# HGRN2's scores inside blocks of 32 and 64 tokens as small column-tiled matmuls

## The reference

```python
cum = jnp.cumsum(gc, axis=2)                                   # gc = log f, f in (0, 1), per token and dimension
diff = cum[:, :, :, None, :] - cum[:, :, None, :, :]
decay = jnp.where(tri, jnp.exp(jnp.where(tri, diff, 0.0)), 0.0)
scores = jnp.einsum('bhtk,bhsk,bhtsk->bhts', qc, kc, decay)    # q_t . k_s, decayed over the tokens between
o = scores @ vc + (qc * exp(cum)) @ S                          # S: state carried from chunk to chunk
```

## Time and profile before

| | |
|---|---|
| timed runs, median (range) | 966.26 us (964.32 to 968.34) |
| profiled execution: its span, first to last instruction | 961.5 us |
| median of the runs less that span | 4.8 us |
| TensorE matmul busy | 932.1 us, 97% |
| VectorE busy | 691.0 us, 72% |
| ScalarE busy | 518.4 us, 54% |
| GpSimd busy | 371.8 us, 39% |
| loads | 162.57 MB, mean 169 GB/s |

### The profile page before, as it was taken

How to read it: one execution, slowest core, us unless ns; L and a number is a source line. 1 busy time by engine, 2 the same in 40 slices (tenths; PEclk the granted TensorE clock), 3 DMA queues, 4 the chain that set the end, 5 groups by cost and what they waited for, 6 DMA issues and landing times.

```text
span 961.5 us, 15057 instructions
## 1 busy us (share of the span) xinstructions
PE 932.1 (97%) x6110; PEld 846.5 (88%) x6110; DVE 691.0 (72%) x886; ACT 518.4 (54%) x790; POOL 371.8 (39%) x136
## 2 busy tenths in 40 slices
PE   7999999999999999999999999999999999999996
PEld 7998986888888878999999999899899888888885
DVE  4998586788884257657688987876645589999722
ACT  6853466544544356655535346555545566666532
POOL 0000000565664410001645542755676345665541
PEclk9999999999999999999999999999999999999998
DMA  9662432755555645445533425344356455555551
GB/s 360 209 214 80 151 129 97 278 176 181 194 196 180 213 154 180 174 157 184 186 108 117 147 89 153 132 135 159 109 182 212 149 197 181 200 189 180 193 197 45
DMA packets 30437, 162.57 MB, mean 169 GB/s; under 512 B 9089, under 2 KB 9489, under 8 KB 11936
## 3 DMA queue, kind: packets, MB, share of 16 engines
q1 hardware_dynamic: 30304, 161.53, 48.7%
q0 software_dynamic: 64, 0.08, 0.0%
HBM read 160.48 MB, written 1.12 MB: 168 GB/s over the span
## 4 chain that ended last, share of the span: by engine, by line
PE 86%; DVE 8%; ACT 3%; DMA 2%; issue 1%; SPq 1%; DVEq 0%; ACTq 0%
PE ring L1582 27%; PE acc L1660 18%; PE acc L1594 9%; PE ring L1594 9%; PE ring L1613 5%; PE acc L1595 4%; PE ring L1595 4%; PE acc L1837 3%; DMA raw<-wstream 2%; PE acc L1695 1%; DVE w_lo L1026 1%; DVE y L1078 1%; ACT w_hi L631 1%; PE ring L1695 1%; DVE ret_inv L1189 1%
## 5 line engine op out<-in xcount | busy, mean ns | idle before, releaser
L594 POOL TENSOR_TENSOR w_lo<-raw,w_hi 128x1024 fp32r<-128x1024 f32 x124 | 358.3, 2894 | 569.5 <-ACT w_hi L631 569.3
L631 ACT CAST w_hi<-raw 128x1024 fp32r<-128x1024 f32 x284 | 296.8, 1051 | 325.2 <-PE ring L1582 127.8
L1026 DVE TENSOR_TENSOR w_lo<-raw,w_hi 128x1024 fp32r<-128x1024 f32 x160 | 198.2, 1250 | 103.2 <-ACT w_hi L631 93.3
L1582 PE MATMUL ring<-h,w_hi 128*128 128x256 f32 x1408 | 257.4, 285 | 5.6 <-DVE w_lo L1026 3.1
L1582 PEld LDWEIGHTS ring<-h,w_hi 128*128 128x128 f32 x1408 | 219.7, 192 | 8.1 <-issue 6.4
L1582 PE MATMUL ring<-h,w_lo 128*128 128x256 f32 x704 | 199.1, 283 | 0.0
L1582 PEld LDWEIGHTS ring<-h,w_lo 128*128 128x128 f32 x704 | 135.0, 192 | 0.0
L1594 PE MATMUL acc<-h,w_hi 128*128 128x512 f32 x352 | 124.7, 397 | 0.8 <-DVE h L1084 0.8
L1594 PE MATMUL ring<-h,w_hi 128*128 128x512 f32 x352 | 124.2, 396 | 0.0
L1595 PE MATMUL acc<-h,w_lo 128*128 128x256 f32 x352 | 98.2, 279 | 0.0
L1595 PE MATMUL ring<-h,w_lo 128*128 128x256 f32 x352 | 98.2, 279 | 0.0
(11 more groups left out here) (255 smaller groups left out, 1395.8 us busy)
## 6 DMA issues: line engine op xcount, KB each, us to landing
raw<-wstream SPq DMA_DIRECT2D x142, 1024.0 KB, 4.9
toep_t<-toep SPq DMA_DIRECT2D x16, 96.0 KB, 3.1
x<-x_tok SPq DMA_DIRECT2D x2, 512.0 KB, 4.9
mem<-mem_tok SPq DMA_DIRECT2D x1, 1024.0 KB, 11.7
w_ple<-wproj SPq DMA_DIRECT2D x1, 1024.0 KB, 7.0
out_t<-y SPq DMA_DIRECT2D x4, 256.0 KB, 2.4
decay<-decay_tab SPq DMA_DIRECT2D x1, 768.0 KB, 6.5
gain_mix_pre<-gains SPq DMA_DIRECT2D x1, 512.0 KB, 6.2
```

What stands on the lines that cost most here:

```text
L594: nc.gpsimd.tensor_tensor(w_lo[:, u % UNITS], unit_of_raw(u), as_f32(w_hi[:, u % UNITS]), ALU.subtract).then_inc(lo_ready["pool"], 1)
L631: nc.scalar.copy(w_hi[:, u % UNITS], unit_of_raw(u)).then_inc(hi_ready, 1)
L1026: V.tensor_tensor(w_lo[:, u % UNITS], unit_of_raw(u), as_f32(w_hi[:, u % UNITS]), ALU.subtract).then_inc(lo_ready["dve"], 1)
L1582: last = mm(dst, w[a], src[:, b, kt], start=n == 0 and i == 0, stop=n == kts - 1 and i == 2)
```

## The change

- The diagonal is computed for blocks of 32 tokens: 64 calls with 32 weight columns and 32 streamed columns, each to its own 32 PSUM partitions, all in one bank. ScalarE copies the bank once, to a compact tile `st_near` of 512 columns (the space of `prod_tmp`).
- Levels 1 to 16 have the same shape (64 calls, one bank each, the banks taken in turn). One masked copy of 128x512 per level brings them into `st_near`; the masks are 32 columns wide and are loaded as 160 columns in place of 896.
- Level 32 (64 calls of 32 columns) and level 64 (32 calls of 64 columns, two banks) compute only the wanted blocks, straight from `k_f`, `k_b`, `q_f`, `q_b`. They have no key copies and no masks.
- ScalarE spreads the scores into `st_hg`: `spread_near` after the last masked level, `spread_far` after levels 32 and 64, each in copies of 32 or 64 partitions with 512 elements a lane, 12 in all.
- `f_f` and `f_b` are one tile, and their product in `grow` is one instruction.
- The cross scores wait for these copies (`st_far`) and for all masked ones.

```diff
-        f_f = at(0, "f_f", HG, S)
-        f_b = at(8, "f_b", HG, S)
+        f_fb = at(0, "f_fb", 2 * HG, S)
+        f_f, f_b = f_fb[:, 0:HG], f_fb[:, HG:]
...
+        st_near = prod_tmp[:].rearrange("p a (n c) -> p (a n) c", c=32)
...
+        def near(lo, n, shift=0):
+            v = st_hg[lo:lo + n].rearrange("p a (b c) -> p a b c", c=P)
+            return v[:, :, 0:4:3, lo % P + shift:lo % P + shift + n]
+
+        def level_bank(i):
+            return sc[(i + 1) % 4]
...
-                if side in LEVEL_AFTER:
+                if LEVEL_AFTER.get(side, MASKED) < MASKED:
                     level_keys(LEVEL_AFTER[side])
...
             def diagonal():
-                for g in range(4):
-                    act.wait_ge(sc_done, SC_LEVEL + g + 1)
-                    nc.scalar.copy(diag_view(g), sc[g][:].rearrange("p (a b c) -> p a b c", a=2, b=2)
-                                   ).then_inc(st_diag, 1)
+                act.wait_ge(sc_done, SC_LEVEL + 1)
+                nc.scalar.copy(st_near.rearrange("p a c -> p (a c)"), sc[0][:]).then_inc(st_diag, 1)
+
+            def spread_near():
+                act.wait_ge(st_mask, MASKED)
+                for lo in range(0, P, 32):
+                    nc.scalar.copy(near(lo, 32), st_near[lo:lo + 32].rearrange("p (a b) c -> p a b c", b=2))
+
+            def spread_far(i):
+                b = LEVELS[i]
+                act.wait_ge(sc_done, SC_LEVEL + 1 + i + 1)
+                banks = [sc[2]] if b == 32 else [sc[3], sc[0]]
+                heads = HG // len(banks)
+                for n, bank_ in enumerate(banks):
+                    for lo in range(0, P, b):
+                        shift = b if lo % (2 * b) == 0 else -b
+                        ins = nc.scalar.copy(near(lo, b, shift)[:, heads * n:heads * n + heads],
+                                             bank_[lo:lo + b].rearrange("p (a b c) -> p a b c", b=2, c=b))
+                    ins.then_inc(st_far, 1)
...
             def masks(i):
-                for g in range(4):
-                    dve.wait_ge(sc_done, SC_LEVEL + 4 * (i + 1) + g + 1)
...
-                    ins.then_inc(st_mask, 1)
+                dve.wait_ge(sc_done, SC_LEVEL + 1 + i + 1)
+                if i >= MASKED:
+                    return
+                if i == 0:
+                    dve.wait_ge(st_diag, 1)
+                c = CONST["mask"] + 32 * i
+                m = con[:, c:c + 32].bitcast(I32).unsqueeze(1).to_broadcast([P, 2 * HG, 32])
+                src = level_bank(i).rearrange("p (a c) -> p a c", c=32)
+                V.copy_predicated(st_near, m, src).then_inc(st_mask, 1)
...
-                V.tensor_tensor(fa[:, :, 0:1], fa[:, :, 0:1], fb_[:, :, 0:1], ALU.mult)
-                V.tensor_tensor(ba[:, :, 0:1], ba[:, :, 0:1], bb_[:, :, 0:1], ALU.mult).then_inc(level_ready, 1)
+                ga, gb = halves(f_fb[:])
+                V.tensor_tensor(ga[:, :, 0:1], ga[:, :, 0:1], gb[:, :, 0:1], ALU.mult).then_inc(level_ready, 1)
...
             def level(i):
                 b = LEVELS[i]
+                w = max(b, 32)
                 pe.wait_ge(level_ready, i + 1)
...
+                if i == 3:
+                    pe.wait_ge(st_diag, 1)
+                if i >= 4:
+                    pe.wait_ge(st_mask, 2 * i - 8 if i == 6 else i - 3)
+                for hd in range(HG):
+                    if i < MASKED and hd % 4 == 0:
+                        pe.wait_ge(mix_keys, 2 * i + hd // 4 + 1)
+                    out_ = level_bank(i + hd // 4 if b == 64 else i)
+                    for tt in range(2):
+                        c = w * ((2 * hd + tt) % (512 // w))
+                        for lo in range(0, P, w):
+                            t = tt * P + lo
+                            if b < 32:
+                                keys = k_mix[hd // 4][:, hd % 4, t:t + w]
+                                queries = partners(q_b[:, hd, t:t + w], b)
+                            elif lo % (2 * b) == 0:
+                                keys, queries = k_f[:, hd, t:t + w], q_f[:, hd, t + b:t + 2 * b]
+                            else:
+                                keys, queries = k_b[:, hd, t:t + w], q_b[:, hd, t - b:t]
+                            last = mm(out_[lo:lo + w, c:c + w], keys, queries, start=True, stop=True)
+                last.then_inc(sc_done, 1)
```

More of the change, by code:

```diff
@@ L172 @@
 LEVELS = [1, 2, 4, 8, 16, 32, 64]
-NCONST = 3 * P + len(LEVELS) * P
+MASKED = 5
+NCONST = 3 * P + MASKED * 32
 def lo_count(u, who):
@@ L373, in program @@
         st_mask = sem("st_mask")
+        st_far = sem("st_far")
         st_cross = sem("st_cross")
@@ L466, in program @@
         SC_LEVEL = 2 * RET
-        SC_CROSS = SC_LEVEL + 4 * (1 + len(LEVELS))
+        SC_CROSS = SC_LEVEL + 1 + len(LEVELS)
         SC_HGO = SC_CROSS + 4
-        def diag_view(g):
-            v = st_hg[:, 2 * g:2 * g + 2].rearrange("p a (b c) -> p a b c", c=P)
-            return v[:, :, 0:4:3]
+        def near(lo, n, shift=0):
[3 more added lines that the diff above has]
+            return sc[(i + 1) % 4]
         SIDE_FILLS = [(name, j) for name, j, _, _ in FILLS if name in ("hi", "hg", "nq", "nk", "nv", "cq")]
@@ L904, in _ @@
                     diagonal()
+                if LEVEL_AFTER.get(e) == MASKED:
+                    spread_near()
+                if LEVEL_AFTER.get(e, 0) >= MASKED:
+                    spread_far(LEVEL_AFTER[e])
                 if e == CROSS_AFTER:
@@ L1361, in grow @@
                 nb = HG * S // (2 * b)
-                fa, fb_ = halves(f_f[:])
-                ba, bb_ = halves(f_b[:])
+                fa, fb_ = halves(f_f)
+                ba, bb_ = halves(f_b)
                 bc = lambda t: t[:, :, 0:1].to_broadcast([P, nb, b])
@@ L1812, in diagonal @@
                 pe.wait_ge(level_ready, 1)
[L1813 to L1819, removed]
+                for hd in range(HG):
+                    for tt in range(2):
+                        c = 32 * (2 * hd + tt)
+                        for lo in range(0, P, 32):
+                            t = slice(tt * P + lo, tt * P + lo + 32)
+                            last = mm(sc[0][lo:lo + 32, c:c + 32], ksum[:, hd, t], q_s[:, hd, t], start=True, stop=True)
@@ L1841, in cross @@
+                last.then_inc(sc_done, 1)
             def cross():
                 pe.wait_ge(level_ready, 1 + len(LEVELS))
+                pe.wait_ge(st_mask, MASKED)
+                pe.wait_ge(st_far, 3)
                 for g in range(4):
-                    pe.wait_ge(st_mask, 4 * (len(LEVELS) - 1) + g + 1)
                     for a in range(2):
@@ L2050, in host_layout @@
     con = [np.eye(P, dtype=f)] + [np.full((P, P), 1.0 / n, f) for n in (512, 128)]
[L2051 to L2054, removed]
+    for b_ in LEVELS[:MASKED]:
+        row, colm = idx[:, None] % 32, idx[None, :32]
+        con.append(((row // (2 * b_) == colm // (2 * b_)) & (row // b_ != colm // b_)).astype(f))
     con = np.concatenate(con, axis=1)
```

## The result

After the change the kernel takes 958.13 us (median of 4 runs, 957.12 to 960.41), the kernel before 966.98 us beside it (4 runs, 964.32 to 968.34). The ratio is 0.9929, 95% interval 0.9907 to 0.9951: faster by 8.9 us, where 20 were forecast. The profiled execution took 957.12 us with a span of 955.3.

What follows compares the result with a forecast made beforehand. TensorE, busy 97% of the span, was taken as the bound. In the stage 37.4 us becomes 14.0 + 2.0 = 16.0, gain 21.4, taken as 20: span 941.5, time 946.3 us, range 939 to 965.

Steps and rivals of the forecast that it cites:

- the 37.4 that the prediction read from the chain: TensorE's chain time for the scores in the stage, outside twelve weight fills; forecast to become 16.0 us.
- The bursts: Score matmuls on TensorE: 1.7 us for each of the first seven groups, 2.1 for level 64, 14.0 us against 29.
- The rival of no overlap: At the bursts, each small record loads, then streams, alone: 55 ns, 7.0 us a level, 987 us; chance 0.12.
- The four updates of 1.2 us stay.: VectorE's four updates per level were forecast to keep their 1.2 us each.
- the merged product: VectorE's f_f and f_b products as one: bounds 3.7 us (one delay) and 6.4 (both); 3.7 used at levels 4 and 8.
- The chain from a burst's end to the next burst: From a burst's end to the first half's keys: 10.3 us, under 11.5 of two fills, so level 4 and 8 gaps go.
- Ahead of level 64: VectorE's chain of 5.1 us, updates and product, hidden under a fill of 5.75; the gap of 1.14 us goes.
- Waits: TensorE's waits in the stage: of 8.4 us some 2.0 were forecast to remain.
- Level 2's: TensorE's wait ahead of level 2, 0.86 us, stays, its keys being queued on ScalarE behind a weight cast.
- The rival in which the gain gets stuck behind the other engines: Merged product of 6.4, slow 32-lane copies or late cast return 1 to 1.5 us per level: 956 us, chance 0.12.
- a wait of up to 1 us for instructions: At the first two groups, 512 instructions in 3 us, TensorE may wait up to 1 us; costed at nothing.
- Carrying 4.8 us around the span: The difference between the 961.5 us span and the 966.26 us median, carried over unchanged to the forecast time.

Runs made afterwards that it cites:

- the first experiment: The kernel after, with every w_lo subtraction of the fills hi 0 to cq 1 on VectorE in place of three in four on GpSimd: 944.90 us, ratio 0.9791.
- both variants of the kernel before: The kernel before, once with every subtraction of the fills hi 0 to cq 1 on VectorE, 964.52 us; once with the two decay products as one instruction, 961.62 us.

## Why the prediction was wrong

Stage, in us: forecast, measured in the kernel after, and in the first experiment.

| | before | forecast | after | all on VectorE |
|---|---|---|---|---|
| bursts and the waits ahead of them | 36.4 | 16.0 | 26.5 | 15.1 |
| stage, diagonal to cross scores | 106.1 | 84.7 | 97.7 | 86.6 |
| gain in the stage | | 21.4 | 8.4 | 19.5 |

(The measured columns are by starts of matmuls; that of before counts 1 us less than the 37.4 that the prediction read from the chain. The waits that the prediction lists add up to 6.8 us of its 8.4; by starts they are 8.0.)

**The bursts: right, and a bit cheap.** Forecast 1.7 us a level, 1.0 for streaming and 0.7 added; the steps of levels 4 to 32 take 1.32 us each in the first experiment, the change of tiling included. The starts lie within 1.10 us. Level 64 was forecast 2.1, and takes that too: its starts lie within 1.86 us, and the change of tiling adds 0.2; in the kernel after, at the low clock, they lie within 2.82. Eight bursts make about 11 us against 14.0. The rival of no overlap is out. The Trainium skill, TensorEngine Tiling (Array Packing), Instruction Overhead, gives every matmul some 60 cycles, by estimate 25 ns at 2.4 GHz; the measured 8.6 ns a record over four tiles is below that, and the measurement decides. Within one tile, with some 33 ns from start to start, it isn't tested here.

**The failed step: "The four updates of 1.2 us stay."** The forecast treated the long f_f and f_b as a property of the products, and bounded only the merged product (3.7 to 6.4 us). That product came out near it at the early levels, 4.4, 2.0 and 3.2 us. But the delay belongs to whatever VectorE runs on two SBUF inputs while GpSimd subtracts. Merging two delayed instructions removed one place to be delayed and moved the delay to the updates. The chain from a burst's end to the next burst, forecast at 10.3 us, is 14.8 before level 4, over the 11.5 us of two fills. Ahead of level 64 it was forecast at 5.1 us under one fill of 5.75, and is 9.1: the first update takes 3.21 us in place of 1.2, and the product, which has 64 elements a lane, 2.30 in place of 0.3. The update ends 1.1 us after a subtraction of GpSimd's, the product lies beside one. The two delays are 4.0 us, more than the 3.25 us of TensorE's wait.

**Waits: forecast 2.0 us, measured about 12.** Ahead of levels 2, 4, 8, 16, 32 and 64 TensorE waits 1.06, 3.23, 1.03, 1.83, 0.47 and 3.25 us, and 1.3 inside level 1 (0.45 for the second key copy, and a stop of 0.85, on which more below). Level 2's is what I said would stay. Those of levels 4, 8 and 64 were to go and didn't; those of 16 and 32, 0.2 us before, are all but new. The rival in which the gain gets stuck behind the other engines, at 956 us, came nearest in time, and in place (1 to 1.5 us a level). Its causes were wrong: neither a product of 6.4, nor slow 32-lane copies, nor a late cast.

**The clock: not in the forecast at all.** The two waits of 3.2 us took it down for 3.4 us each. Between starts the fills of the stage cost 1.4 us more than before. Two more falls, near 135 and 599 us, cost 1.6 and 1.5 us. The one at 135 isn't the change's: it stands behind a wait of 2.2 us that is the same in all 13 profiled executions, and came in 7 of them, both variants of the kernel before among them. The one at 599 stands behind a wait of 2.0 us that all 13 have too, and came in two of them. And 0.8 us were gained near 40 us, where a wait of 1.5 us for VectorE is missing. That wait comes and goes as well: the two variants of the kernel before, with the old constants, don't have it, and three variants of the kernel after do. These three take the stage's 8.4 to about the 6.2 us between the spans; by the medians it is 8.9.

**The rest.** ScalarE's copies are hidden, as forecast. The masked copies are five of 0.75 us against 0.7. The cross scores don't wait for VectorE's updates. The instruction queue went from 0.80 to 0.88 MB against 90 KB forecast. For the first two groups the forecast allowed a wait of up to 1 us for instructions, and something stops TensorE there:

```profile
476.72 0.62 PE L1870 MATMUL acc<-q_bf,k_mix 128*32 128x32 f32 x37 [0.85 <-issue]
```

The stop comes behind record 219 of the 256 of the diagonal and level 1, where the program waits for nothing. It stands at the same record in the kernel after and in all eight variants of it that keep the interleaved order, 0.5 to 1.8 us long, and not in the one ordered tile by tile, whose bursts are slower. That fits instructions that arrive late, but no run here shows the cause. Carrying 4.8 us around the span was wrong in a small way: the runs show 1.8 to 1.9 between span and time, so the profiled execution of before comes to some 963.3 us, under the three runs shown with it.

Taken together: the work removed from TensorE was worth about what I said, and became visible (944.9 us against the forecast 946.3) only when VectorE was let off its waits for GpSimd. That the two numbers lie so close is in part luck: the bursts are some 3 us cheaper than forecast there, the waits 2 us dearer, and the fills, with the stop at 506.6 us in one, 1.8 us dearer.

**Open.** The stop inside level 1, and the one inside a fill of the first experiment; why the clock falls behind the waits at 132 and 597 us in some executions and not in others.

## What to carry to other kernels

When an instruction is long for its elements, find what it collides with before costing it: a delay that belongs to two engines doesn't go with the instruction that shows it, it moves to the next one in its place. Work that reads PSUM can be the cover under which GpSimd runs for free; if you shrink it, redo the timetable of GpSimd, or try giving VectorE the work outright. Put small column-tiled matmuls in the queue so that neighbours go to different tiles, and look at the clock behind the waits of TensorE: they can cost twice. Before you ascribe a difference between two profiled executions to the change, look for it in the other kernels' executions.

## What the runs showed of the hardware

- An update of 1.2 us takes up to 3.43 us beside GpSimd's subtraction, which takes 2.38 us alone and up to 3.3 beside VectorE. A masked copy with its data in PSUM takes 0.74 to 0.75 us with or without GpSimd.
- Float32 records of 32 by 32 columns: 8.6 ns each with four column tiles interleaved (about 33 ns from one to the next of a tile), 26 to 27 ns each when ordered tile by tile.
- Behind TensorE's waits of 3.2 us the granted clock was 0.5 for 3.4 us, twice in the stage; 12 small matmuls in each gap kept it at 1.00. Behind a wait of 2.2 us at 132 us it fell in 7 of 13 profiled executions, behind one of 2.0 us at about 597 us in 2 of 13.
